# Hybrid encoder block on one core: the inverse deviation by Ln, Exp and a Newton step, and a new order of the norm's steps in each pass

## The reference, cut to what matters

```python
xn = rms_norm(x, norm_mix_g)
z = xn @ w_in                    # columns [B | C | h | q | k | v], 512 each
u = C * h                        # causal convolution of width 3 per channel
y_conv = B * (conv3(u) + conv_b)
q, k = rms_norm(q, q_gain), rms_norm(k, k_gain)      # per head, 64 wide
p = softmax(q @ k_band.T / 8 + rel_bias)             # 64-row chunks, band of 9 chunks
y_attn = p @ v_band
y_mix = concat(group_norm(y_conv, 64), group_norm(y_attn, 64))
h = x + y_mix @ w_out
out = h + square(relu(rms_norm(h) @ w_mlp_in)) @ w_mlp_out
```

## Time and profile before

| | us |
|---|---|
| median of three runs | 1195.67 |
| the three runs | 1195.95, 1193.72, 1195.67 |
| the profiled execution's own time | 1192.94 |
| its span (first to last instruction) | 1191.0 |
| busy PE / DVE / POOL / ACT | 1131.7 / 762.8 / 629.2 / 533.7 |
| mean granted clock of PE | 0.991 |

### The profile page before, as it was taken

How to read it: one execution, slowest core, us unless ns; L and a number is a source line. 1 busy time by engine, 2 the same in 40 slices (tenths; PEclk the granted TensorE clock), 3 DMA queues, 4 the chain that set the end, 5 groups by cost and what they waited for, 6 DMA issues and landing times.

```text
span 1191.0 us, 14699 instructions
## 1 busy us (share of the span) xinstructions
PE 1131.7 (95%) x5368; PEld 938.1 (79%) x5368; DVE 762.8 (64%) x860; ACT 533.7 (45%) x835; POOL 629.2 (53%) x349
## 2 busy tenths in 40 slices
PE   4999999999999989998799999999998999999998
PEld 4778878877887877787688888888877888888887
DVE  7567867876786787444343443435358677776788
ACT  5454454455446464313445444454544333343331
POOL 3421240322124012035668888878769699696892
PEclk9999999999999999899999999999999999999999
DMA  7210110111010142220245444444487635445324
GB/s 230 92 53 18 50 49 11 53 37 35 18 51 22 50 167 90 102 72 36 62 141 195 141 165 145 159 159 142 136 287 267 211 106 170 151 134 197 110 87 159
DMA packets 98512, 135.81 MB, mean 114 GB/s; under 512 B 8072, under 2 KB 52112, under 8 KB 98456
## 3 DMA queue, kind: packets, MB, share of 16 engines
q1 hardware_dynamic: 95104, 131.13, 32.9%
q10 hardware_dynamic: 3352, 3.94, 1.1%
HBM read 97.27 MB, written 39.34 MB: 115 GB/s over the span
## 4 chain that ended last, share of the span: by engine, by line
PE 79%; issue 8%; DVE 5%; POOL 3%; ACT 2%; DMA 1%; SPq 0%; DVEq 0%; POOLq 0%; ACTq 0%
PE PJ L1473 15%; PE SC L1727 9%; PE PJ L1727 9%; PE OS L1727 7%; PE PJ L1764 6%; PE PT L1764 6%; PE SC L1764 6%; PE OS L1764 6%; PE PJ L1549 5%; PE SC L1507 3%; PE OS L1531 2%; PE PT L1518 1%; POOL wsl L506 1%; DVE sq L1016 1%; POOL wsl L504 1%
## 5 line engine op out<-in xcount | busy, mean ns | idle before, releaser
L1473 PE MATMUL PJ<-actT,wsl 128*128 128x512 f32 (+1 forms) x1176 | 299.8, 398 | 2.4 <-POOL wsl L506 2.4
L1473 PEld LDWEIGHTS PJ<-actT,wsl 128*128 128x128 f32 x1176 | 211.8, 192 | 40.8 <-POOL wsl L506 2.8
L616 POOL TENSOR_TENSOR ring<-b,ring 128x1024 fp32r<-128x1024 f32 x48 | 137.8, 2879 | 37.8 <-ACT ring L944 37.6
L1382 DVE TENSOR_TENSOR ring<-hraw,ring 128x1024 fp32r<-128x1024 f32 x56 | 151.3, 2738 | 3.8 <-ACT ring L939 3.8
L504 POOL CAST wsl<-raw 128x1024 fp32r<-128x1024 f32 x24 | 26.9, 1121 | 199.6 <-PE PJ L1473 183.9
L939 ACT ACTIVATE ring<-hraw 128x1024 fp32r<-128x1024 f32 x56 | 59.2, 1058 | 134.4 <-PE OS L1764 62.6
L1727 PE MATMUL OS<-actT,w1a 128*128 128x512 f32 x384 | 93.4, 391 | 1.7 <-ACT p1s L880 1.7
L723 ACT ACTIVATE prob<-prob,negm 128x640 f32<-128x640 f32 (+4 forms) x64 | 44.6, 697 | 107.9 <-DVE negm L1090 107.7
L1764 PE MATMUL PJ<-ring 128*128 128x512 f32 x336 | 82.2, 395 | 6.1 <-POOL ring L616 4.5
L1016 DVE RECIPROCAL sq<-sq 128x256 f32<-128x256 f32 (+1 forms) x43 | 82.5, 1925 | 3.9 <-ACT sq L690 3.9
L1727 PEld LDWEIGHTS OS<-actT,w1a 128*128 128x128 f32 x384 | 71.6, 188 | 16.5 <-POOL w1a L557 1.9
(11 more groups left out here) (193 smaller groups left out, 2227.7 us busy)
## 6 DMA issues: line engine op xcount, KB each, us to landing
hraw<-hidd SPq DMA_DIRECT2D x56, 512.0 KB, 3.6
w1r<-in_w_mlp_in SPq DMA_DIRECT2D x16, 1024.0 KB, 6.1
hidd<-hs SPq DMA_DIRECT2D x64, 256.0 KB, 2.0
b<-in_w_mlp_out SPq DMA_DIRECT2D x16, 1024.0 KB, 6.5
raw<-in_w_in SPq DMA_DIRECT2D x24, 512.0 KB, 3.7
hidd<-h SPq DMA_DIRECT2D x48, 256.0 KB, 2.3
xin<-in_x SPq DMA_DIRECT2D x8, 512.0 KB, 8.5
woraw<-in_w_out SPq DMA_DIRECT2D x8, 512.0 KB, 7.5
```

The source lines that it names most:

```text
L616: nc.gpsimd.tensor_tensor(duo(n)[1][LO], W2_SRC[name][:, 2 * d:2 * d + 2], duo(n)[1][HI].bitcast(F32), ALU.subtract).then_inc(s["wl2_done" ...
L1382: vec.tensor_tensor(duo(n)[0][LO], hraw[:, n % HRING], duo(n)[0][HI].bitcast(F32), ALU.subtract).then_inc(s["hl2_done"], 1)
L1473: last = mm(PJ[:, g % 2, cols], wsl[:, w % NSLOT, a, k], actT[:, b, k, c], start=(r == 0), stop=(r == 3 * KD - 1))
```

## The change

1. `deviation` makes 1 / sqrt in ACT: r0 = exp(-0.5 ln(`SS` / 64 + eps)) and `rt` = r0 squared / 128, that is Ln, Exp and Square, each waiting for the one before. `rt` lies on the memory of `sql`. `inverse` then makes one Newton step on DVE: `rt` = (`SS` + 64 eps) * `rt`, and `sq` = (`rt` - 1.5) * r0. The result is negative, so the convolution's gain is negated once; in q and k the two signs cancel. `SS` is now freed (`ss_read`) by the first of the two DVE steps. POOL waits for `rsc_done` before it writes `sql`.
2. `o_dev` becomes Ln and Exp, and `o_norm` three small steps in place of one reciprocal.
3. In each pass PE makes `sum_squares(2)` at "2a" (before "1b") and `sum_squares(3)` at "4a" ("3b"). ACT: `deviation(2)` in unit 2, ahead of `take(3)`; `v_copy(1)` alone in unit 3; `qk_hi(2)`, `deviation(3)` in unit 4; `qk_hi(3)` behind `c_copy(0)` in unit 5. DVE: `inverse(2)` whole at "3a", `squares_lo(3)` at "3b", `qk_scale(2)` at "4a", `inverse(3)` whole at "5a", `qk_scale(3)` and `qk_lo(2)` at "5b", `qk_lo(3)` at "6b", `v_lo(1)` at "7a".
4. The copy of `prm` and the halo's zeroing go to "2b" (`prepare`).
5. Prologue: another interleaving of `x_scale`, low parts, `x_hi` and transposes; the last four transposes stand inside groups 1 and 2, the sums of squares of n = 0, 1 in group 2; POOL converts the second weight once `x_scale(3)` is done, and zeroes `qz` behind the third weight.

```diff
@@ allocation
+        rt = nc.alloc_sbuf_tensor_at("rt", [P, 2, HALF], F32, offset=top[0])
         sql = put("sql", [P, 2, HALF], F32R)
@@ POOL, weights
+                    if w == 1 and first:
+                        pool.wait_ge(s["xs_done"], 4)
...
+                    if w == 2 and first:
+                        pool.wait_ge(s["tr_done"], NT)
+                        pool.wait_ge(s["w_ready"], 3)
+                        for slot in QZ:
+                            nc.gpsimd.memset(qz[HEADS[0], :, slot, :].bitcast(F32), 0.0).then_inc(s["qz_zero"], 1)
+                        pool.wait_ge(s["qz_zero"], len(QZ))
                     if w == 2:
                         pool.wait_ge(s["sqh_done"], it * 6 + 2)
+                        pool.wait_ge(s["rsc_done"], it * 2 + 1)
...
-                    if w == 1 and first:
-                        pool.wait_ge(s["tr_done"], NT)
-                        pool.wait_ge(s["w_ready"], 2)
-                        for slot in QZ:
-                            nc.gpsimd.memset(qz[HEADS[0], :, slot, :].bitcast(F32), 0.0).then_inc(s["qz_zero"], 1)
-                        pool.wait_ge(s["qz_zero"], len(QZ))
@@ ACT
             for t in range(NT):
                 x_stats(t)
-                if t >= 2:
+                if 2 <= t < 6:
                     x_hi(t - 2)
...
-                act.activation(sq[:, zbuf(n)], SS[:, :], ACT.Sqrt, bias=eps[:, 0:1], scale=1.0 / HD).then_inc(s["ss_read"], 1)
+                act.activation(sq[:, zbuf(n)], SS[:, :], ACT.Ln, bias=eps[:, 0:1], scale=1.0 / HD).then_inc(s["dev_done"], 1)
+                act.wait_ge(s["dev_done"], it * 18 + 3 * n + 1)
+                act.activation(sq[:, zbuf(n)], sq[:, zbuf(n)], ACT.Exp, scale=-0.5).then_inc(s["dev_done"], 1)
+                act.wait_ge(s["dev_done"], it * 18 + 3 * n + 2)
+                act.activation(rt[:, n % 2], sq[:, zbuf(n)], ACT.Square, scale=(0.5 / HD) ** 0.5
+                               ).then_inc(s["dev_done"], 1)
...
                     if u == 0:
                         take(it, 2)
-                    if u == 1:
+                    if u == 2:
                         deviation(it, 2)
-                    if u == 2:
                         take(it, 3)
                     if u == 3:
+                        v_copy(it, 1)
+                    if u == 4:
                         qk_hi(it, 2)
-                        v_copy(it, 1)
                         deviation(it, 3)
-                    if u == 4:
+                    if u == 5:
                         v_hi(it, 1)
-                    if u == 5:
+                        c_copy(it, 0)
                         qk_hi(it, 3)
-                        c_copy(it, 0)
...
             take(0, 0)
-            x_hi(NT - 2)
-            x_hi(NT - 1)
+            x_hi(4)
+            x_hi(5)
+            take(0, 1)
+            x_hi(6)
             deviation(0, 0)
-            take(0, 1)
+            x_hi(7)
             deviation(0, 1)
@@ DVE
-            for t in range(NT):
+            for t in range(3):
                 x_scale(t)
-                if t >= 2:
-                    dve.wait_ge(s["xhi_done"], t - 1)
-                    lo_part(t - 2, slice((t - 2) * P, (t - 1) * P))
+            x_lo(0)
+            x_scale(3)
+            for t in range(1, 4):
+                x_lo(t)
+            for t in range(4, NT):
+                x_scale(t)
...
+                r0, w = sq[:, zbuf(n)], rt[:, n % 2]
                 if part != 1:
+                    dve.wait_ge(s["dev_done"], it * 18 + 3 * n + 3)
+                    vec.scalar_tensor_tensor(w, SS[:, :], HD * EPS, w, ALU.add, ALU.mult).then_inc(s["ss_read"], 1)
+                if part != 0:
                     dve.wait_ge(s["ss_read"], it * 8 + (TURN[n] + 3 + extra))
-                op = vec.reciprocal(sq[:, b, c], sq[:, b, c])
-                if part != 0:
-                    op.then_inc(s["rs_done" if n < 4 else "rsc_done"], 1)
+                    vec.scalar_tensor_tensor(r0, w, 1.5, r0, ALU.subtract, ALU.mult).then_inc(s["rs_done" if n < 4 else "rsc_done"], 1)
...
                 if at == "1a":
                     squares_lo(it, 2)
-                if at == "2a":
+                if at == "2b":
+                    prepare(it)
+                if at == "3a":
                     inverse(it, 2, 0)
-                if at == "2b":
                     inverse(it, 2, 1)
-                if at == "3a":
-                    qk_scale(it, 2)
+                if at == "3b":
                     squares_lo(it, 3)
                 if at == "4a":
+                    qk_scale(it, 2)
+                if at == "5a":
                     inverse(it, 3, 0)
-                if at == "4b":
                     inverse(it, 3, 1)
-                if at == "5a":
+                if at == "5b":
                     qk_scale(it, 3)
-                if at == "5b":
                     qk_lo(it, 2)
-                if at == "6a":
+                if at == "6b":
                     qk_lo(it, 3)
-                if at == "6b":
+                if at == "7a":
                     v_lo(it, 1)
-                if at == "7a":
                     conv_gate(it, 0)
@@ PE
-                    if at == "1b":
+                    if at == "2a":
                         sum_squares(it, 2)
-                    if at == "3b":
+                    if at == "4a":
                         sum_squares(it, 3)
...
             for r in range(3 * KD):
+                if r in (4, 14):
+                    x_transpose(4 + r // 8)
+                group_product(0, 1, r, first=True)
+            for r in range(3 * KD):
+                if r in (2, 12):
+                    x_transpose(6 + r // 8)
+                if r == 6:
+                    sum_squares(0, 0, 1)
+                if r == 20:
+                    sum_squares(0, 1, 1)
                 group_product(0, 2, r)
```

More of the change, by code:

```diff
@@ L210, in build @@
         sm_done ptlo_done rl_done osc_done osq_done oss_done ors_done on_done
-        zs_done sq_done sqh_done hi_done vcopy_done cs_done vhi_done exp_done pthi_done ss_read osd_done
+        zs_done dev_done sq_done sqh_done hi_done vcopy_done cs_done vhi_done exp_done pthi_done ss_read osd_done
         wohi_done wo_ready woq_ready ymhi_done ym_ready mix_done hadd_done wlast_done
@@ L732, in o_dev @@
                 act.wait_ge(s["oss_done"], it * 2 + (g + 1))
-                act.activation(osd[:, :], oss[:, :], ACT.Sqrt, bias=eps[:, 0:1], scale=1.0 / HD).then_inc(s["osd_done"], 1)
+                act.activation(osd[:, :], oss[:, :], ACT.Ln, bias=eps[:, 0:1], scale=1.0 / HD).then_inc(s["osd_done"], 1)
+                act.wait_ge(s["osd_done"], it * 4 + (2 * g + 1))
+                act.activation(osd[:, :], osd[:, :], ACT.Exp, scale=-0.5).then_inc(s["osd_done"], 1)
             def o_store(it, g):
@@ L968, in _ @@
             vec = nc.vector
+            dve.sem_inc(s["rsc_done"], 1)
             vec.memset(eps[:, :], EPS).then_inc(s["masks_ok"], 1)
@@ L998, in _, with x_lo @@
             dve.wait_ge(s["g_in"], 16)
-            for t in range(NT):
+            def x_lo(t):
+                dve.wait_ge(s["xhi_done"], t + 1)
+                lo_part(t, slice(t * P, (t + 1) * P))
+            for t in range(3):
                 x_scale(t)
-                if t >= 2:
-                    dve.wait_ge(s["xhi_done"], t - 1)
-                    lo_part(t - 2, slice((t - 2) * P, (t - 1) * P))
+            x_lo(0)
[4 more added lines that the diff above has]
+                x_scale(t)
             def squares_lo(it, n):
@@ L1071, in conv_scale @@
             def conv_scale(it, n):
-                dve.wait_ge(s["rsc_done"], it * 2 + (n + 1))
+                dve.wait_ge(s["rsc_done"], it * 2 + (n + 2))
                 vec.scalar_tensor_tensor(ymix[:, 4 * n:4 * n + 4, bass.ds(it, 1), :].rearrange("p t o c -> p t (o c)"),
@@ L1132, in o_norm @@
             def o_norm(it, g):
-                dve.wait_ge(s["osd_done"], it * 2 + (g + 1))
-                vec.reciprocal(ors[:, :], osd[:, :]).then_inc(s["ors_done"], 1)
-                dve.wait_ge(s["ors_done"], it * 2 + (g + 1))
+                dve.wait_ge(s["osd_done"], it * 4 + (2 * g + 2))
+                vec.scalar_tensor_tensor(ors[:, :], oss[:, :], HD * EPS, osd[:, :], ALU.add, ALU.mult).then_inc(s["ors_done"], 1)
+                dve.wait_ge(s["ors_done"], it * 6 + (3 * g + 1))
+                vec.scalar_tensor_tensor(ors[:, :], ors[:, :], -0.5 / HD, osd[:, :], ALU.mult, ALU.mult).then_inc(s["ors_done"], 1)
+                dve.wait_ge(s["ors_done"], it * 6 + (3 * g + 2))
+                vec.scalar_tensor_tensor(ors[:, :], ors[:, :], 1.5, osd[:, :], ALU.add, ALU.mult).then_inc(s["ors_done"], 1)
+                dve.wait_ge(s["ors_done"], it * 6 + (3 * g + 3))
                 vec.tensor_tensor(og[:, g], og[:, g], per_unit(ors), ALU.mult).then_inc(s["on_done"], 1)
@@ L1213, in extras, with prepare @@
                     inverse(it, 5, 1)
```

(29 more changed lines are left out.)

2 lines of the change are left out of this document (removed).

## The result

The changed kernel takes 1217.13 us (median of four runs, 1216.07 to 1218.01) against 1194.7 us for the kernel before on the same chip: ratio 1.0188, 95% interval 1.0170 to 1.0206. It is 1.9% slower. The prediction said 1185.5 us and gave 0.87 to "faster"; the time lies above its range and 7 us above rival 3's 1210.

What follows compares the result with a forecast made beforehand. TensorE, busy 95% of the span, was taken as the bound, so only its waits counted. Terms 2.4 + 2.6 + 2.7 + 2.1 + 0.4 + 0 = 10.2 us, taken from 1195.67, gave 1185.5 us; range 1178 to 1192.

Steps and rivals of the forecast that it cites:

- rival 3: Tables switch inside each deviation: two loads each, PE waits 3.0 us at group 6; 14 us slower, 1210; chance 0.07.
- Deviation: ACT's Sqrt becomes Ln, Exp, Square: 1.3 us more each time, both 1.28 us table loads per visit taken as gone.
- Four passes: Units 2 to 7: the sum_squares(3) wait shrinks, a new 1.35 us wait forms at score(8); 2.4 us won in all.
- Clock: Slow PE stretches of passes 0 and 2, behind the old 2.1 us wait, go: 2.6 us won.
- Rival 2: The new wait at score(8) costs the clock as the old did, in all four passes: 5.2 us, 1190.7; chance 0.12.
- Parameters: At pass starts, the prm copy moved to "2b" no longer meets L506 or delays score(1): 2.7 us won.
- The tap: Last pass, unit 13: conv_tap(1,0) starts some 0.2 us ahead of POOL's L535 and is not held; 2.1 us, or 0.
- Tail: Mixer's end: o_transpose(1) waits 2.7 us, but later waits for normalised rows shrink; 0.4 us won, bounds -1.5 and +1.9.
- Prologue: Before the first scores: first products earlier and a 2.43 us wait gone, but new waits come; 0, bounds -2.4 and +2.4.
- Inverse: DVE's 3.34 us reciprocal becomes two 0.75 us steps, 1.8 us less for each of six per pass; second held if meeting L506.

Runs made afterwards that it cites:

- e1: The changed kernel plus one line loading a table set that holds both exp and ln before the first take; 1176.62 us, ratio 0.9849 to the kernel before.
- e6: e1 with qk_lo(3), the low part of k, moved from "6b" back to "6a", ahead of pt_lo(6); 1171.1 us, ratio 0.9802 to the kernel before.
- e7: e1 with the copy of prm and the halo's zeroing put back in front of scores(0); 1182.13 us, ratio 0.9893 to the kernel before.
- e8: e1 with the start of the kernel put back in the old order on all engines; 1179.67 us, ratio 0.9858 to the kernel before.
- e4: e1 with the two table loads put back into deviation(2) and deviation(3) alone; 1199.65 us, ratio 1.0025 to the kernel before.
- e2: The kernel before, in its old order and prologue, with the new Ln, Exp, Square form and the joint set loaded once; 1188.13 us, ratio 0.9956.

## Why the prediction was wrong, point by point

**The step that failed** stands in *Deviation*: "I take both as gone, as no Sqrt is left in the passes". No Sqrt is left, but the loads are not gone; they doubled, from 32 to 64. In the trace one of 1.283 us stands in front of each of the 24 Ln and each of the 24 Exp of the deviations, so two different sets took turns. Nor do they "hide in ACT's idle time", as the loads of before were said to: they stand in front of `take(3)` and of `inverse(3)`, where PE waits. A set that holds both exists, and e1 shows that one explicit load of it keeps every later one out of the passes, which is worth 40.5 us. The prediction did see that no row could tell this, gave the way out as rival 3, and put 0.07 on it. That chance leaned on the page "ScalarE activation tables: per-element evaluation and per-set limits" (Table sets in the compiler and the runtime) of the Trainium skill, by which the loads are placed by the greedy longest run. The trace does not bear out what the prediction drew from it: in e1 Ln, Exp, Square, copies and exponentials go through the passes on the joint set without a load, and in the changed kernel 64 loads stand among the same functions.

**Rival 3's steps** against the trace. `take(3)` late and 3.0 us of wait at group 6: measured 2.99, four times. `inverse(3)` waits for ACT in unit 5: it does (1.44 us), and this makes the wait at `score(8)` 2.06 us, 1.23 more than in e1, where 1.3 more was put. The pass's end late by 2: its three waits are 4.1 us, 3.8 more than in e1, at three ends. The rival gave 1210 and the kernel takes 1217; the pass's end is the term that was too small, by 5.4 us, and the clock was left out (0.50 behind group 6 in passes 0 and 3 of the changed kernel).

**The sum, measured where its premise holds.** e1 is the kernel that the prediction summed: the same change with no load in the passes. Its median lies at 1176.6, where the sum had 1185.5 and the range began at 1178, so with the loads away the sum would still have been too cautious. In spans e1 won 16.0 us (1191.0 to 1175.0) and not 10.2; most of the other 3.1 us is that the sum was set on a median 2.7 us above the profiled execution. The table sets places of PE's queue side by side (us from the start; gain since the place above).

| place | before | changed | e1 | gain of e1 | gain by the sum |
|---|---|---|---|---|---|
| sum of n=4, pass 0 | 112.65 | 115.13 | 107.82 | 4.8 | 1.8 |
| the same, pass 1 | 215.33 | 224.14 | 208.37 | 2.1 | 1.0 |
| the same, pass 2 | 321.01 | 333.12 | 308.91 | 5.1 | 4.0 |
| `prob_v` behind `o_sum(5)` | 438.29 | 462.58 | 423.67 | 2.5 | 3.0 |
| first transpose of the second norm | 481.71 | 507.23 | 465.52 | 1.6 | 0.4 |
| end | 1191.0 | 1216.0 | 1175.0 | -0.2 | 0 |

- *Four passes (2.4).* Two passes of 0.65 and two of 0.5 make 2.3, not 2.4. Right in mechanism, too small: about 1.2 us more in each. `score(8)` waits 0.83 and not 1.35 us, `sum_squares(3)` 0.22 and not 0.1, group 6 0.29 and not 0.45. About 0.6 us of each pass is in no wait that the trace lists; where it comes from is open. The new wait is real, and e6 removes it.
- *Clock (2.6).* Right for the profiled executions: e1's windows have 1.00 from 50 to 430 us, in all four passes. Rival 2 (a loss behind the 0.83 us waits) did not come.
- *Parameters (2.7).* Right: the wait is gone. In the new order the copy would have cost 5.3 us (e7), where `score(1)` waits 2.24 us in two passes.
- *The tap (2.1).* Wrong: the tap started 0.05 us ahead of L539 (0.2 was put) and was held all the same, 2.70 us against 0.54 for one that nothing holds. PE waits 1.72 us in e1, so 0.4 is won:

```profile
420.49 2.70 DVE L1077 TENSOR_SCALAR zs<-ub,prm 128x512 f32<-128x512 f32 x1
420.54 2.37 POOL L539 TENSOR_TENSOR wo<-woraw,wo 128x1024 fp32r<-128x1024 f32 x1 [3.72 <-ACT wo L771]
423.11 0.41 DVE L1138 TENSOR_REDUCE on<-OS 128x128 f32<-128x256 f32 x1
```

- *Tail (0.4).* 1.6 measured. `o_transpose(1)` waits 0.60 us and not 2.7, another 1.56 is lost at a `wo` of POOL's, and the last transposes wait 0.38 in the place of 2.77.
- *Prologue (0).* Worth 1.1 to 3.6 us (e8); the upper end lies outside the bound of 2.4. The wait in front of the second sum of squares is 2.31 us in e1 and for `rt`, where 1.4 behind POOL's zeroing was put.
- *Inverse.* Confirmed: 0.69 us for each step. The second one is held when it meets POOL, as the prediction allowed (2.16 us at 169.10 above), and the step after it was ready in time.

## What to carry to other kernels

Before a function on ScalarE is exchanged for a pair of others, ask what table loads stand between the two. That they could share a set does not mean that they do, and one explicit load of the joint set was worth 40.5 us here. A long step in a queue costs by what is queued behind it: the same loads cost half as much where the deviation did not stand ahead of the copy that frees PE's bank. Two edits that each leave one wait standing can show little alone (0.1%, which is within the noise, and 0.4%) and much together (1.5%), so judge them in a grid and not one at a time.

## What the runs showed of the hardware that was not expected

- A table load costs little besides its 1.283 us. From the start of Ln to that of Exp it is 2.00 us in the changed kernel (177.16 to 179.16) and 0.71 in e1 (163.70 to 164.41), so the load adds 1.29. From the start of the copy before it to that of Ln it is 1.70 (175.46 to 177.16) against 0.28 (163.42 to 163.70), so the load adds 1.42; about 0.1 of that is the overlap of two neighbours, which e1 has there and the changed kernel has not.
- A DVE instruction with a single tensor in SBUF as its input (the tap, 128x512) was held to 2.70 us beside POOL's subtraction, although its recorded start is 0.05 us the earlier one. The Trainium skill's page "SBUF — State Buffer" (SBUF: two separate sides) says that, of the DVE and GpSimd instructions that contend for the shared ports, the one that starts first gets them for its whole instruction. The recorded starts do not agree with that, but they are so near that the trace cannot tell who asked first.
- The same wait does not always cost the clock. In the 3 us behind the 2.99 us at group 6 the changed kernel shows a granted clock of 0.50, that is 1.2 GHz, in passes 0 and 3 (from 71.5 and 399.8 us) and 1.00 in passes 1 and 2 (from 182 and 291 us). e4 has the same wait at the same place and shows 0.65 in pass 0 (from 69.2 us) and 0.50 in the other three. It varies between executions of one kernel too: the nine of e2 have a mean clock of 0.987 to 0.994 and take 1194.33 to 1187.46 us, so a difference of 2 or 3 us between single executions says little.
